# Three pairs of expert slots in rotation, and a tail that adds the last rows in two fp32r parts, in a hybrid diffusion step with 32 routed experts

## The chip, the cores and the metric

The kernel runs as one program on one core of a Trainium2 chip. The metric is the device time of one execution in microseconds (us), as the median of three runs. The engines are TensorE (PE, with PEld for its weight loads), VectorE (DVE), ScalarE (ACT), GpSimd (POOL) and SyncE (SP), which issues most of the transfers; 16 DMA engines carry them. Each engine runs its own list of instructions in order, and the lists are tied together by semaphores alone.

## What is computed

One layer of a diffusion backbone over 128 context tokens and 512 latent tokens of width 1024: normalisation, retention and differential attention, their merge, a residual, and then a mixture of experts and the final norm. The change touches only the last part, which in the reference is:

```python
combine = jnp.einsum('nk,nke->ne', w, jax.nn.one_hot(gidx, N_EXPERTS, dtype=F32))    # top 2 of 32 experts
a = jax.nn.silu(jnp.einsum('nd,edf->nef', hf, wg)) * jnp.einsum('nd,edf->nef', hf, wu)
y = jnp.einsum('nef,efd->nd', a * combine[:, :, None].astype(a.dtype), wd)
...
x = x + g2 * hier_moe(h2, rgw, rgb, rew, reb, wg, wu, wd)
y_prompt = rmsnorm(xp, final_norm_g)
y_sample = rmsnorm(xs, final_norm_g)
```

All inputs and outputs are float32. An expert has three weights of 1 MB each (gate, up and down; 1024 by 256, twice, and 256 by 1024).

## The kernel before

The 640 tokens are five tiles of 128 rows (`NT = 5`; `PT = 4` is the context tile). The residual `x1` stays in SBUF. The normalised rows `h2` are written to a table in DRAM, and routing on the chip gives each expert 64 places. Experts are worked in 16 **pairs** (`PAIRS`), expert 2p and 2p+1 sharing the 128 places of pair p. For each pair:

- POOL gathers the pair's rows from the table (`rows_in`, L2423) into `xg`;
- PE transposes them (`gathered`, L1319), ACT copies them out (L1711);
- PE multiplies by the gate and up weights (`gate_up`, L1326) as soon as `ld_gu` says that they have landed; ACT and DVE form silu times up, times the routing weight (L1716, L2264, L2269);
- PE transposes that (`hidden`, L1332), ACT copies it (L1720), and PE multiplies by the down weights (`down`, L1339);
- DVE multiplies by the modulation row `g2` into `y_out` (`gated_rows`, L2279) and signals `y_d`; POOL scatters `y_out` to the table `y_rows` in DRAM (`rows_out`, L2428) and signals `st_y`. The last pair is not scattered: the tail adds it from `y_out` by a one-hot matrix `last_hot`.

SBUF holds weights of six experts, in **slots** 0 to 5 (`w_gu`, `w_dn`). SP loads them in program order. Pairs 0, 1 and 2 are loaded into slots 0-1, 2-3 and 4-5 ahead of time. Then only slots 0-1 and 2-3 take turns: `next_weights(p, e, slot)` waits until PE is through with the gate and up weights of pair p and loads the next two experts there, then the same for the down weights. Slots 4-5 stand idle from pair 2 until pair 13, whose experts are loaded there after the loop, one expert after the other (gate, up, down of 26, then of 27). Pairs 14 and 15 go to slots 0-1 and 2-3: gate and up of both first (pair 15's in two halves, L918, the second half signalling `ld_rest`), then down of both. PE's code matches this: pairs 3 to 12 are a hardware loop over two pairs, and for pairs 14 and 15 it runs `gate_up` of 15 before `down` of 14.

**The tail.** When all of `y_rows` is stored (`st_y`, waited for by SP at L932) SP loads two rows for each token, `y1` and `y2` (L949, L950), in order of tiles, each pair of them signalling `ld_y[t]`. PE puts into PSUM `last_hot * y_out` (`last_rows`, L1436) and `identity * y2` (`second_rows`, L1441), all in float32, first `last_rows` of four tiles and then `second_rows` of four. For each tile DVE adds `y1` to `x1` (L2331), then PSUM to `x1` (L2333), then multiplies by the final norm's row (L2335); ACT sums the squares (L1762), POOL takes the inverse root (L2401, L2402), ACT scales (L1758) and SP stores (L954).

Code behind `n_over > 0` serves experts with more than 64 rows; it is not entered with these inputs.

## Time and profile before

| what | value |
|---|---|
| median of 3 runs | 1228.64 us (1227.13 to 1230.97) |
| the profiled execution | 1228.74 us, of which the span is 1226.9 us |
| PE busy | 1082.7 us, 88% of the span |
| DVE, ACT, POOL busy | 594.7, 403.2, 104.7 us |
| mean rate of the DMA engines | 184 GB/s over the span |
| moved in the span | 226.09 MB |

The span is the time between the first and the last instruction that the profiler recorded; 1.8 us of the execution lie around it. Busy shares are means over stages with different limits, so the stage that the change touches (from about 950 us to the end) has to be read by itself: who waits there, and for what. Only the waits on the path that ends last cost time.

### The profile page before, as it was taken

The page shows a single profiled execution, that of the slowest core. Times are in us where ns is not written, and L with a number is a line of the kernel's source. Part 1 is how long each engine was busy: PE and PEld are TensorE (multiplying, and loading weights), DVE is VectorE, ACT ScalarE, POOL GpSimd, SP SyncE. Part 2 cuts the span into 40 slices and gives each one's busy share as a digit, 9 for nine tenths or more (in the row PEclk, how much of TensorE's full clock was granted, in tenths as well). Part 3 has the DMA queues.
Part 4 walks back from the last instruction along what each step waited for, and adds up shares of the span by engine and source line. Part 5 has one row for each costly group of instructions (what it writes and reads, how often), then busy time and mean ns, then how long its engine had stood idle before and what let it go on. Part 6 is the DMA issues. An engine that isn't in the chain of part 4 may idle for free.

```text
span 1226.9 us, 13934 instructions
## 1 busy us (share of the span) xinstructions
PE 1082.7 (88%) x5427; PEld 772.2 (63%) x5427; DVE 594.7 (48%) x927; ACT 403.2 (33%) x797; POOL 104.7 (9%) x106
## 2 busy tenths in 40 slices
PE   3999999989999999999998899799993998777785
PEld 2687777777887777777876666687883333222232
DVE  3478525647335454451536665455559322122125
ACT  4441131112245565562236565341331111011103
POOL 1000011111000000000000101000014011111002
PEclk9999999989999999999999999899995999999898
DMA  8757723211421212213230211563618989999966
GB/s 301 263 169 258 263 93 119 71 60 52 146 86 54 92 52 91 82 61 120 77 121 9 66 52 52 216 270 131 240 52 317 388 342 424 421 421 421 417 247 253
DMA packets 72317, 226.09 MB, mean 184 GB/s; under 512 B 9533, under 2 KB 20086, under 8 KB 58562
## 3 DMA queue, kind: packets, MB, share of 16 engines
q1 hardware_dynamic: 64722, 208.35, 46.0%
q0 software_dynamic: 4464, 10.12, 2.2%
q10 hardware_dynamic: 3072, 6.82, 1.5%
q8 instruction: 40, 0.66, 0.2%
q14 instruction: 19, 0.16, 0.0%
HBM read 205.68 MB, written 25.72 MB: 189 GB/s over the span
## 4 chain that ended last, share of the span: by engine, by line
PE 61%; DVE 10%; DMA 9%; issue 8%; ACT 8%; SPq 2%; POOL 1%; ACTq 0%; DVEq 0%; POOLq 0%
PE ps L1090 36%; PE ps L1326 8%; DMA arena<-in_moe_w_up 6%; PE ps L1250 3%; PE ps L1339 3%; ACT arena L1663 3%; DMA arena<-in_w_ada 2%; PE ps L1280 2%; ACT w_high L1482 1%; PE ps L1264 1%; DVE mx L2128 1%; DVE w_low L1833 1%; DVE mx L2129 1%; PE ps L1121 1%; SPq L671 1%
## 5 line engine op out<-in xcount | busy, mean ns | idle before, releaser
L1090 PE MATMUL ps<-w_high,h_high 128*128 128x512 f32 x600 | 242.1, 404 | 5.1 <-DVE arena L1944 2.2
L1090 PE MATMUL ps<-w_high,h_low 128*128 128x512 f32 x600 | 235.6, 393 | 0.0
L1090 PE MATMUL ps<-w_low,h_high 128*128 128x512 f32 x600 | 235.5, 392 | 0.0
L1833 DVE TENSOR_TENSOR w_low<-w_loaded,w_high 128x2048 fp32r<-128x2048 f32 x44 | 100.7, 2289 | 107.2 <-ACT w_high L1482 107.1
L1326 PE MATMUL ps<-arena 128*64 128x512 f32 x512 | 121.5, 630 | 23.5 <-DMA arena<-in_moe_w_up 15.8
L1090 PEld LDWEIGHTS ps<-w_high,h_high 128*128 128x128 f32 x600 | 114.0, 190 | 34.6 <-issue 6.4
L1090 PEld LDWEIGHTS ps<-w_high,h_low 128*128 128x128 f32 x600 | 113.8, 190 | 24.8
L1090 PEld LDWEIGHTS ps<-w_low,h_high 128*128 128x128 f32 x600 | 114.1, 190 | 22.5
L1482 ACT CAST w_high<-w_loaded 128x2048 fp32r<-128x2048 f32 x44 | 84.0, 1910 | 76.6 <-DMA w_loaded<-in_w_in 42.9
L1326 PEld LDWEIGHTS ps<-arena 128*64 128x64 f32 x512 | 39.1, 145 | 103.6 <-issue 103.2
L1591 ACT COPY arena<-ps 128x512 f32<-128x512 f32 x55 | 32.3, 587 | 168.0 <-PE ps L1090 168.0
L1663 ACT ACTIVATE arena<-ps,neg_mx 128x768 f32<-128x768 f32 (+1 forms) x80 | 62.9, 792 | 41.1 <-DVE neg_mx L2130 40.9
L1716 ACT ACTIVATE arena<-ps 128x256 f32<-128x256 f32 x16 | 6.2, 385 | 196.4 <-PE ps L1326 196.4
L2264 DVE SCALAR_TENSOR_TENSOR arena<-arena,ps 128x256 f32<-128x256 f32 x16 | 6.7, 421 | 128.1 <-ACT arena L1716 128.1
L1339 PE MATMUL ps<-arena 128*64 128x512 f32 x256 | 58.4, 598 | 9.9 <-ACT arena L1720 8.7
L1250 PE MATMUL ps<-arena 64*128 64x256 f32 (+2 forms) x288 | 54.7, 494 | 7.2 <-ACT arena L1663 5.7
L2128 DVE TENSOR_REDUCE mx<-ps 128x1 f32<-128x768 f32 (+1 forms) x40 | 32.8, 821 | 40.9 <-PE ps L1250 40.9
L1280 PE MATMUL ps<-arena 128*128 128x128 f32 x384 | 48.0, 275 | 0.0
L1280 PEld LDWEIGHTS ps<-arena 128*128 128x128 f32 x384 | 46.4, 192 | 1.1
L1886 DVE SCALAR_TENSOR_TENSOR arena<-arena 128x2048 f32<-128x2048 f32 x20 | 45.8, 2346 | 1.4 <-DMA arena<-in_w_ada 1.4
L2279 DVE TENSOR_TENSOR arena<-ps,arena 128x1024 f32<-128x1024 f32 x16 | 19.6, 1224 | 53.7 <-PE ps L1339 29.7
L1264 PE MATMUL ps<-const,arena 128*128 128x128 f32 x200 | 30.8, 286 | 16.5 <-ACT ps L1680 14.1
(300 smaller groups left out, 1657.8 us busy)
## 6 DMA issues: line engine op xcount, KB each, us to landing
arena<-in_moe_w_down SPq DMA_DIRECT2D x32, 1024.0 KB, 19.4
arena<-in_moe_w_gate SPq DMA_DIRECT2D x30, 1024.0 KB, 13.4
arena<-in_moe_w_up SPq DMA_DIRECT2D x30, 1024.0 KB, 18.0
w_loaded<-in_w_in SPq DMA_DIRECT2D x27, 1024.0 KB, 5.9
arena<-in_w_ada SPq DMA_DIRECT2D x24, 1024.0 KB, 5.7
w_loaded<-in_w_in ACTq DMA_DIRECT2D x5, 1024.0 KB, 7.4
y_rows<-arena SPq DMA_DIRECT2D x10, 512.0 KB, 7.0
gates<-arena SPq DMA_DIRECT2D x20, 256.0 KB, 2.0
```

The costliest lines, as they stand in the source:

```text
L1090: mm = pe.matmul(out, x[:, t, kk * P:(kk + 1) * P], w[w_buf(i)][:, k, :], start=(begins and k == 0 and j == 0), stop=(k == HK - 1 and j == ...
L1250: mm = pe.matmul(score[c][:, lo:hi], qT[h % 2][r, t * P:(t + 1) * P], keys, start=True, stop=True, skip_group_check=True)
L1264: mm = pe.transpose(B(6 + k // 4)[:, (k % 4) * P:(k % 4 + 1) * P], mixed[:, k * P:(k + 1) * P], ident)
L1280: mm = pe.matmul(pv_out, mixedT[s % 2][:, k * P:(k + 1) * P], v, start=(k == 0), stop=(k == 5))
L1326: mm = pe.matmul(B(bank_at)[BLK * i:BLK * (i + 1), :].rearrange("p (g f) -> p g f", g=2), xgT[slot][:, k, BLK * i:BLK * (i + 1)], w_gu[e0 ...
L1339: mm = pe.matmul(B(5 + n)[BLK * i:BLK * (i + 1), :], act_aT[slot][:, k, BLK * i:BLK * (i + 1)], w_dn[e0 + i][:, k, n * N512:(n + 1) * N512 ...
L1482: act.copy(w_hi[w_buf(i)][:], w_raw[w_buf(i)]).then_inc(w_rounded, 1)
L1591: free(act.copy(dst[:, t, c0:c0 + N512], src), n)
L1663: act.activation(probs[:, c, 0:n], score[c][:, 0:n], ACT.Exp, bias=neg_mx[:, s % 2, c:c + 1], scale=DH ** -0.5, accum_out=den[:, s % 2, c: ...
L1833: dve.tensor_tensor(w_lo[b][:], w_raw[b], w_hi[b][:].bitcast(F32), ALU.subtract).then_inc(w_split, 1)
L1886: ins = dve.scalar_tensor_tensor(out=total, in0=ada_place[i % 2], scalar=ccol[:, k, s:s + 1], in1=total, op0=ALU.mult, op1=ALU.add)
L2128: dve.tensor_reduce(mx[:, 0:1], score[0][:, 0:n], AXX, ALU.max)
```

## The change

It does four things.

1. The six slots rotate as three pairs of slots: pair p uses slots 2(p mod 3) and the next, throughout. SP's loop becomes written-out code: for p from 3 to 14 it waits until PE is through with the gate and up weights of pair p-3, loads those of p, waits for the down product of pair p-3, loads the down weights of p. Pair 15 has its halves as before, in slots 0-1. PE's loop is written out as well.
2. PE's order at the end: pair 14 is an ordinary pair, and pair 15 follows it whole. DVE and ACT follow suit.
3. `y1`, `y2` and `fin_row` get other places in SBUF. The load of `fin_row` waits for the down product of pair 13 and no longer for its gate and up product.
4. The tail: ACT rounds the last pair's rows to fp32r (`y_high`, two halves), DVE makes the rest (`y_low`), and `last_rows` is now two fp32r products, with `y_high` and `y_low`, in place of one in float32. In each tile `second_rows` comes first; the order on PE is second 0, second 1, last 0, last 1, then second and last tile by tile. DVE adds `y1` two tiles ahead.

```diff
-        fin_row = at(162, D)
-        y1, y2 = tiles(28, NT, D), tiles(48, NT, D)
+        fin_row = at(102, D)
+        y1, y2 = tiles(118, NT, D), tiles(158, NT, D)
+        y_high, y_low = split_at("y_high", 86, 1, D), split_at("y_low", 90, 1, D)
...
-        last_hot = masks[:, 0:NT * P]
+        last_hot = nc.alloc_sbuf_tensor_at("last_hot", [P, NT * P], F32R, offset=masks_base)
...
+            for p in range(3, PAIRS - 1):
+                slot = 2 * (p % 3)
+                sp.wait_ge(pe_gu, p - 2)
                 for i in range(2):
-                    load_gate_up(e + i, slot + i)
-                sp.wait_ge(pe_dn, p + 1)
+                    load_gate_up(2 * p + i, slot + i)
+                sp.wait_ge(pe_dn, p - 2)
                 for i in range(2):
-                    load_down(e + i, slot + i)
-
-            next_weights(0, 6, 0)
-            next_weights(1, 8, 2)
-            with sp.Fori(0, (PAIRS - 8) // 2) as i:
-                next_weights(2 * i + 3, 4 * i + 10, 0)
-                next_weights(2 * i + 4, 4 * i + 12, 2)
-
-            for e, slot in ((NE - 6, 4), (NE - 5, 5)):
-                load_expert(e, slot)
-            sp.wait_ge(pe_gu, PAIRS - 4)
-            for i in range(2):
-                load_gate_up(NE - 4 + i, i)
...
-            sp.wait_ge(pe_gu, PAIRS - 2)
+            sp.wait_ge(pe_dn, PAIRS - 2)
             sp.dma_start(fin_row, a["final_norm_g"].partition_broadcast(P)).then_inc(ld_fin, 16)
...
+            for p in range(PAIRS - 1):
+                pair(p, p % 2, 2 * (p % 3), p // 2, p // 3, first=(p == 0))
...
-            def last_rows(t):
-                for n in range(2):
-                    pe.matmul(B(2 * t % 8 + n), last_hot[:, t * P:(t + 1) * P], y_out[:, 1, n * N512:(n + 1) * N512], start=True, stop=False)
-
             def second_rows(t):
                 pe.wait_ge(ld_y[t], 16 + 32)
                 for n in range(2):
-                    mm = pe.matmul(B(2 * t % 8 + n), ident, y2[:, t, n * N512:(n + 1) * N512], start=False, stop=True)
+                    pe.matmul(B(2 * t % 8 + n), ident, y2[:, t, n * N512:(n + 1) * N512], start=True, stop=False, skip_group_check=True)
+
+            def last_rows(t):
+                for n in range(2):
+                    c = slice(n * N512, (n + 1) * N512)
+                    pe.wait_ge(y_split, split_before + n + 1)
+                    for y in (y_high, y_low):
+                        mm = pe.matmul(B(2 * t % 8 + n), last_hot[:, t * P:(t + 1) * P], y[:, 0, c], start=False, stop=(y is y_low), skip_group_check=True)
                 mm.then_inc(pe_sum, 1)
...
+            second_rows(0)
+            second_rows(1)
+            last_rows(0)
+            last_rows(1)
+            pe.wait_ge(y_d, PAIRS)
+            for t in range(2, PT):
+                second_rows(t)
                 last_rows(t)
-            for t in range(PT):
-                second_rows(t)
             pe.wait_ge(x2_ready, 1)
+            second_rows(PT)
             last_rows(PT)
-            second_rows(PT)
...
+            act.wait_ge(y_d, PAIRS)
+            for n in range(2):
+                c = slice(n * N512, (n + 1) * N512)
+                act.copy(y_high[:, 0, c], y_out[:, 1, c]).then_inc(y_rounded, 1)
...
+                dve.tensor_tensor(y_low[:, 0, c], y_out[:, 1, c], y_high[:, 0, c].bitcast(F32), ALU.subtract).then_inc(y_split, 1)
...
+            first_rows(0)
+            first_rows(1)
             dve.wait_ge(ld_fin, 16 * 3)
             for t in range(NT):
-                dve.wait_ge(ld_y[t], 16 + 32)
-                link(dve.tensor_tensor(x1[:, t, :], x1[:, t, :], y1[:, t, :], ALU.add))
-                dve.wait_ge(pe_sum, t + 1)
-                dve.tensor_tensor(x1[:, t, :], x1[:, t, :], psf[:, (2 * t % 8) * N512:(2 * t % 8 + 2) * N512], ALU.add).then_inc(x2_ready, 1)
-                dve.wait_ge(x2_ready, t + 1)
-                dve.tensor_tensor(y1[:, t, :], x1[:, t, :], fin_row, ALU.mult).then_inc(fin_scaled, 1)
+                last_sum(t)
+                if t + 2 < NT:
+                    first_rows(t + 2)
+                scaled_by_norm(t)
```

On PE, the end of the expert stage, from pair 13's `gate_up` to pair 15's `down`, reads as follows before (L1326 `gate_up`, L1319 `gathered`, L1332 `hidden`, L1339 `down`):

```order
L1326 MATMUL ps<-arena 64x512 x16
L1319 MATMUL ps<-const,arena 128x128 x8
L1332 MATMUL ps<-const,arena 128x128 x2
L1339 MATMUL ps<-arena 64x512 x8
L1326 MATMUL ps<-arena 64x512 x16
L1319 MATMUL ps<-const,arena 128x128 x8
L1332 MATMUL ps<-const,arena 128x128 x2
L1326 MATMUL ps<-arena 64x512 x16
L1339 MATMUL ps<-arena 64x512 x8
L1332 MATMUL ps<-const,arena 128x128 x2
L1339 MATMUL ps<-arena 64x512 x8
```

The same stretch of the changed kernel (L1316 `gate_up`, L1309 `gathered`, L1322 `hidden`, L1329 `down`):

```order
L1316 MATMUL ps<-arena 64x512 x16
L1309 MATMUL ps<-const,arena 128x128 x8
L1322 MATMUL ps<-const,arena 128x128 x2
L1329 MATMUL ps<-arena 64x512 x8
L1316 MATMUL ps<-arena 64x512 x16
L1309 MATMUL ps<-const,arena 128x128 x8
L1322 MATMUL ps<-const,arena 128x128 x2
L1329 MATMUL ps<-arena 64x512 x8
L1316 MATMUL ps<-arena 64x512 x16
L1322 MATMUL ps<-const,arena 128x128 x2
L1329 MATMUL ps<-arena 64x512 x8
```

Pair 14's `down` has moved ahead of pair 15's `gate_up`. On SP, the loads behind the loop, that is for pairs 13, 14 and 15, stood before as follows (L793 gate and up, L796 down, L918 the halves of pair 15):

```order
L793 DMA arena<-in_moe_w_gate 128x2048
L793 DMA arena<-in_moe_w_up 128x2048
L796 DMA arena<-in_moe_w_down 128x2048
L793 DMA arena<-in_moe_w_gate 128x2048
L793 DMA arena<-in_moe_w_up 128x2048
L796 DMA arena<-in_moe_w_down 128x2x1024
...
L918 DMA arena<-in_moe_w_gate 128x1024
L918 DMA arena<-in_moe_w_up 128x1024
L796 DMA arena<-in_moe_w_down 128x2048 x4
L927 DMA arena<-in_final_norm_g 128x1024
```

In the changed kernel the same stretch, from the down weights of pair 13 on, is (L797 gate and up, L800 down, L911 the halves):

```order
L800 DMA arena<-in_moe_w_down 128x2048 x2
L797 DMA arena<-in_moe_w_gate 128x2048
L797 DMA arena<-in_moe_w_up 128x2048
L797 DMA arena<-in_moe_w_gate 128x2048
L797 DMA arena<-in_moe_w_up 128x2048
L800 DMA arena<-in_moe_w_down 128x2048
L800 DMA arena<-in_moe_w_down 128x2x1024
L911 DMA arena<-in_moe_w_gate 128x1024
...
L800 DMA arena<-in_moe_w_down 128x2048 x2
L917 DMA arena<-in_final_norm_g 128x1024
```

Pair 14's two down loads now stand ahead of pair 15's gate and up loads, and only pair 15's two down loads stand behind those. In the tail, DVE's rows from the first sum on were before (L2331 adds `y1`, L2333 adds PSUM, L2335 multiplies), three for each of five tiles, of which the first two tiles are shown:

```order
L2331 TENSOR_TENSOR arena<-arena 128x1024
L2333 TENSOR_TENSOR arena<-arena,ps 128x1024
L2335 TENSOR_TENSOR arena<-arena 128x1024
L2331 TENSOR_TENSOR arena<-arena 128x1024
L2333 TENSOR_TENSOR arena<-arena,ps 128x1024
L2335 TENSOR_TENSOR arena<-arena 128x1024
```

and of the changed kernel (L2313, L2317, L2321 the same three), up to the second tile's product:

```order
L2313 TENSOR_TENSOR arena<-arena 128x1024 x2
L2317 TENSOR_TENSOR arena<-arena,ps 128x1024
L2313 TENSOR_TENSOR arena<-arena 128x1024
L2321 TENSOR_TENSOR arena<-arena 128x1024
L2317 TENSOR_TENSOR arena<-arena,ps 128x1024
L2313 TENSOR_TENSOR arena<-arena 128x1024
L2321 TENSOR_TENSOR arena<-arena 128x1024
```

Two additions of `y1` now stand ahead of the first sum with PSUM, so that from the start of the first of those sums to the start of the last DVE has eleven instructions to run, where it had twelve.

## Rows read from the trace of the kernel before

**Rows 1.** The page, second part: 40 equal slices of 30.7 us.

```profile
PEclk9999999989999999999999999899995999999898
GB/s 301 263 169 258 263 93 119 71 60 52 146 86 54 92 52 91 82 61 120 77 121 9 66 52 52 216 270 131 240 52 317 388 342 424 421 421 421 417 247 253
```

**Rows 2.** Three stretches: length; PE busy, instructions; clock; DMA share; GB/s.

```profile
992.00:1001.00 9.00, 8.34 (x44) 1.00 0.51 163
1001.00:1179.00 178.00, 142.05 (x643) 0.95 1.02 419
1179.00:1191.00 12.00, 10.90 (x52) 1.00 0.31 128
```

**Rows 3.** The timeline of PE's gate and up products (start, length, what, idle before).

```profile
1048.34 8.78 PE L1326 MATMUL ps<-arena 128*64 128x512 f32 x32 [3.03 <-DMA arena<-in_moe_w_up]
1065.69 7.09 PE L1326 MATMUL ps<-arena 128*64 128x512 f32 x32 [1.96 <-DMA arena<-in_moe_w_up]
1153.66 9.06 PE L1326 MATMUL ps<-arena 128*64 128x512 f32 x32 [6.35 <-issue]
```

**Rows 4.** Pair 14's up weights, second expert: its issue and landing.

```profile
L793 SPq DMA_DIRECT2D arena<-in_moe_w_up x1: 3198/3198/3198, 1139.8 to 1139.8; - x1
...
DMA to landing us min/median/max: 28.4/28.4/28.4
```

**Rows 5.** Pair 15's last up half: its issue and landing.

```profile
L918 SPq DMA_DIRECT2D arena<-in_moe_w_up x1: 2141/2141/2141, 1160.5 to 1160.5; - x1
...
DMA to landing us min/median/max: 19.0/19.0/19.0
```

**Rows 6.** The scatters of pairs 3 to 13, and that of pair 14.

```profile
L2428 POOL DMA_INDIRECT y_rows<-arena,to_idx x11: 1011/1011/1011, 1007.1 to 1170.6; - x11
DMA to landing us min/median/max: 7.9/8.5/8.9
L2428 POOL DMA_INDIRECT y_rows<-arena,to_idx x1: 1923/1923/1923, 1190.3 to 1190.3; - x1
DMA to landing us min/median/max: 4.2/4.2/4.2
```

**Rows 7.** The timeline from 1165 us on, its main steps.

```profile
1165.36 3.65 PE L1339 MATMUL ps<-arena 128*64 128x512 f32 x16 [0.46 <-ACT arena L1720]
1170.63 1.01 POOL L2428 DMA_INDIRECT y_rows<-arena,to_idx  x1 [19.25 <-DVE arena L2279]
1178.14 7.09 PE L1326 MATMUL ps<-arena 128*64 128x512 f32 x32 [0.18 <-ACT arena L1711]
1190.26 1.92 POOL L2428 DMA_INDIRECT y_rows<-arena,to_idx  x1 [18.62 <-DVE arena L2279]
1193.88 1.22 DVE L2279 TENSOR_TENSOR arena<-ps,arena 128x1024 f32<-128x1024 f32 x1 [2.57 <-PE ps L1339]
1194.73 0.33 SPq L949 DMA_DIRECT2D arena<-y_rows  x1
1201.20 1.23 DVE L2331 TENSOR_TENSOR arena<-arena 128x1024 f32<-128x1024 f32 x1 [6.10 <-DMA arena<-y_rows]
1202.54 5.71 PE L1441 MATMUL ps<-arena,const 128*128 128x512 f32 x12
1204.52 1.22 DVE L2333 TENSOR_TENSOR arena<-arena,ps 128x1024 f32<-128x1024 f32 x1 [2.10 <-PE ps L1441]
1219.12 1.22 DVE L2333 TENSOR_TENSOR arena<-arena,ps 128x1024 f32<-128x1024 f32 x1
```

**Rows 8.** The second load of tile 1, `y2`: its issue and landing.

```profile
L950 SPq DMA_DIRECT2D arena<-y_rows x1: 433/433/433, 1196.1 to 1196.1; - x1
...
DMA to landing us min/median/max: 7.6/7.6/7.6
```

**Rows 9.** PE in a dense stretch where all is fp32r products (L1090).

```profile
560.00:570.00 10.00, 10.00 (x46) 1.00 0.22 84
```

**Rows 10.** The queue that brings instructions: packets, MB, share.

```profile
q8 instruction: 40, 0.66, 0.2%
```

More of the change, by code:

```diff
@@ L282, in build @@
         lam_s, neg_lam = sb("lam_s", [P, 2]), sb("neg_lam", [P, 1])
+        masks_base = -(-nc.sbuf_base // 32) * 32
         masks = sb("masks", [P, 12 * P])
@@ L917, in _ @@
                     for g, w in enumerate((a["moe_w_gate"], a["moe_w_up"])):
-                        sp.dma_start(w_gu[2 + i][:, g, ks, :], w[0, NE - 2 + i].rearrange("(p k) f -> p k f", p=P)[:, ks, :]).then_inc(ld_rest if half else ld_gu[2 + i], 16)
-            sp.wait_ge(pe_dn, PAIRS - 4)
-            for i in range(2):
-                load_down(NE - 4 + i, i)
+                        sp.dma_start(w_gu[i][:, g, ks, :], w[0, NE - 2 + i].rearrange("(p k) f -> p k f", p=P)[:, ks, :]).then_inc(ld_rest if half else ld_gu[i], 16)
             sp.wait_ge(pe_dn, PAIRS - 3)
             for i in range(2):
-                load_down(NE - 2 + i, 2 + i)
-            sp.wait_ge(pe_gu, PAIRS - 2)
+                load_down(NE - 2 + i, i)
+            sp.wait_ge(pe_dn, PAIRS - 2)
             sp.dma_start(fin_row, a["final_norm_g"].partition_broadcast(P)).then_inc(ld_fin, 16)
@@ L1373, in _ @@
             gathered(0).then_inc(pe_xt, 1)
-            pair(0, 0, 0, 0, 0, first=True)
-            pair(1, 1, 2, 0, 0)
-            pair(2, 0, 4, 1, 0)
-            with pe.Fori(0, (PAIRS - 6) // 2) as i:
-                pair(2 * i + 3, 1, 0, i + 1, i + 1)
-                pair(2 * i + 4, 0, 2, i + 2, i + 1)
-            h = PAIRS // 2 - 1
-            pair(PAIRS - 3, 1, 4, h - 1, 1)
-            a_p, b_p = PAIRS - 2, PAIRS - 1
-            for i in (0, 1):
-                pe.wait_ge(ld_gu[i], 32 * h)
-            pe.wait_ge(xt_read, a_p + 1)
-            gate_up(0, 0, 2).then_inc(pe_gu, 1)
-            pair_gathered(b_p, 1, h)
-            pe.wait_ge(gu_act, a_p + 1)
-            hidden(0).then_inc(pe_aT, 1)
-            pe.wait_ge(xt_read, b_p + 1)
-            for i in (2, 3):
-                pe.wait_ge(ld_gu[i], 32 * h)
+            for p in range(PAIRS - 1):
+                pair(p, p % 2, 2 * (p % 3), p // 2, p // 3, first=(p == 0))
+            p = PAIRS - 1
+            for i in (0, 1):
+                pe.wait_ge(ld_gu[i], 32 * (p // 3) + 32)
+            pe.wait_ge(xt_read, p + 1)
             for half in range(2):
@@ L1396, in _ @@
                     pe.wait_ge(ld_rest, 64)
-                mm = gate_up(1, 2, 3, range(HK * half, HK * half + HK))
+                mm = gate_up(1, 0, 3, range(HK * half, HK * half + HK))
             mm.then_inc(pe_gu, 1)
-            pe.wait_ge(aT_read, a_p + 1)
+            pe.wait_ge(gu_act, p + 1)
+            hidden(1).then_inc(pe_aT, 1)
+            pe.wait_ge(aT_read, p + 1)
             for i in (0, 1):
-                pe.wait_ge(ld_dn[i], 16 * h)
-            pe.wait_ge(y_d, a_p)
-            down(0, 0).then_inc(pe_dn, 1)
-            pe.wait_ge(gu_act, b_p + 1)
-            hidden(1).then_inc(pe_aT, 1)
-            pe.wait_ge(aT_read, b_p + 1)
-            for i in (2, 3):
-                pe.wait_ge(ld_dn[i], 16 * h)
-            pe.wait_ge(y_d, b_p)
-            down(1, 2).then_inc(pe_dn, 1)
+                pe.wait_ge(ld_dn[i], 16 * (p // 3) + 16)
+            pe.wait_ge(y_d, p)
+            down(1, 0).then_inc(pe_dn, 1)
             n_over = pe.value_load(n_ov[0:1, 0:1], min_val=0, max_val=OVER)
-            pe.wait_ge(y_d, PAIRS)
             with pe.If(n_over > 0):
+                pe.wait_ge(y_d, PAIRS)
                 with pe.Fori(0, OVER // 2) as j:
@@ L2301, in _ @@
             pair(1, 1, 0, first=True)
-            with dve.Fori(1, PAIRS // 2 - 1) as i:
+            with dve.Fori(1, PAIRS // 2) as i:
                 for par in range(2):
                     pair(2 * i + par, par, i)
-            for par in range(2):
-                pair_act(PAIRS - 2 + par, par)
-            for par in range(2):
-                pair_rows(PAIRS - 2 + par, par, PAIRS // 2 - 1)
+            for n in range(2):
+                c = slice(n * N512, (n + 1) * N512)
+                dve.wait_ge(y_rounded, rounded_before + n + 1)
+                dve.tensor_tensor(y_low[:, 0, c], y_out[:, 1, c], y_high[:, 0, c].bitcast(F32), ALU.subtract).then_inc(y_split, 1)
             n_over = dve.value_load(n_ov[0:1, 0:1], min_val=0, max_val=OVER)
```

16 lines of the change are left out of this document (13 added, 3 removed).

## The prediction

> **What bounds the kernel now.** I read the page's slices first, then the granted clock and DMA share by stretches, then the timeline of the last 80 us, and last the landing times of single transfers. The slices show two regimes: TensorE at full clock and 50 to 270 GB/s mostly up to slice 30, and from slice 34 to 38 some 421 GB/s in every slice, and 0.8 is the lowest granted clock of a slice behind slice 31 [rows 1]. Between 1001 and 1179 us all 16 DMA engines are busy (share 1.02) at 419 GB/s, while PE is busy 142 of 178 us [rows 2]. That stage waits for weights: `gate_up` of pair 7 had PE idle for 3.03 us until an up weight landed, and then took 8.78 us in place of 7.09, because the granted clock had fallen to its lower level (1.2 GHz) [rows 3]. So a PE that is done sooner gains nothing there; a DMA engine that is busy sooner does.
>
> Ahead of that stage lies a hole. From 992 to 1001 us the DMA share is 0.51 at 163 GB/s [rows 2]: slots 4-5 are free after pair 2, but SP loads nothing into them. The lost DMA time is 9.0 x (1 - 0.51/1.02) = 4.5 us.
>
> The end is a chain through three engines. Pair 14's scatter is issued at 1190.26 and lands 4.2 us later [rows 6, 7]; the first load of `y1` leaves at 1194.73; tile 0 can be added at 1201.20; the first sum with PSUM starts at 1204.52, the last at 1219.12, and from there 7.8 us of square, root, scale and store lead to the span's end [rows 7]. I call the start of the first `y1` load **Y**. It is late because pair 14's `down` stands behind pair 15's `gate_up` (1178.14 to 1185.2).
>
> **The change, step by step.**
>
> *Filled hole.* After the change pair 5 is loaded when pair 2's `gate_up` is done, with pairs 3 and 4 still in the queue, so the hole closes and every later weight moves forward. Mean over the engines: 4.5 us. But engines differ: at the end they run out over 12 us (share 0.31 from 1179 to 1191 [rows 2]), and a transfer has landed only when its slowest engine is through. The slowest ones had less of a hole to fill. Bounds 0 and 4.5; I take s = 4.0, near the upper end, because the hole is longer than the spread could have become in a stage this short before it.
>
> The Trainium skill (DMA: Bandwidth & Descriptors, section "Latency and other measured facts") says that DMA engines 7 and 15 are usually slower than the others in traces. That would agree with the tail of the share; by it s would be well under the mean hole, and the forecast would come out up to 4 us later, which is rival B.
>
> *Pair 14.* Its last gate/up transfer landed at 1139.8 + 28.4 = 1168.2 [rows 4]. The bytes ahead of it are the same in both orders, so it lands at 1164.2, and `gate_up` starts at 1164.4 (pair 13's weights, now gate and up first, are no obstacle). From a start of `gate_up` to the issue of the scatter there is 7.09 us [rows 3], then about 2.6 us to `down`, 3.65 us of `down` [rows 7], and 1.7 us to DVE's product and POOL's issue. For pair 13, cold, it was 1170.63 - 1153.66 = 17.0 us [rows 3, 7]; less the 2.0 us by which its `gate_up` was long (9.06 against 7.09), 15.0 us. The scatter is issued at 1164.4 + 15.0 = 1179.4. If PE idles 3 us or more ahead of it and the clock falls, 1.7 us later. The wait of about 3 us per pair at 16 to 17 us for weights against 13 us for work decides this; in the trace cold and warm pairs take turns [rows 3]. I take half: 1180.2.
>
> *The scatter's flight.* Between 7.9 and 8.9 us with busy DMA engines, 4.2 us when they are nearly idle [rows 6]. Now it falls into the stretch in which engines run out one after the other (1179 to 1191 us before, so about 1175 to 1187). Bounds 4.2 and 8.9; I take 7.2, nearer the busy end, because it has landed only when the slowest engine has carried its part. With the 0.27 us from landing to issue (1190.26 + 4.2 = 1194.46 to 1194.73), Y = 1180.2 + 7.2 + 0.3 = 1187.7. That is 7.0 us earlier.
>
> *Pair 15 must not be later than that.* Its last up half landed at 1160.5 + 19.0 = 1179.5 with 4.2 MB of down weights behind it [rows 5]; now 2.1 MB of those are ahead, 5.0 us at 419 GB/s, so 1179.5 + 5.0 - 4.0 = 1180.5. `gate_up` starts when `down` of 14 is over, at 1164.4 + 7.1 + 2.6 + 3.65 = 1177.8 (warm) or 1179.5 (cold); its second half 3.5 us later, so nothing waits. `down` of 15 then ends at about 1191.2 to 1192.9 (before: 1193.8), DVE's product 1.3 us later. ACT's two copies and DVE's two subtractions, of 512 columns each at some 0.6 us, are done by 1194 to 1196. In the new order they are needed when `second_rows` of tiles 0 and 1 are through, after 1197. Cost 0; had Y come at 1184 they would begin to show.
>
> *The start of the tail.* The loads of `y1` and `y2` are the same 5.2 MB. Before, the first sum started at Y + 9.8. Now `last_rows(0)` stands behind `second_rows(1)`, and that waits for tile 1, which lands at 1196.1 + 7.6 = 1203.7, that is Y + 9.0 [rows 8]. Then `second_rows(1)`: 12 instructions take 5.71 us for three tiles [rows 7], so 1.8 us with the drain; then four fp32r products of 10/46 = 0.22 us each [rows 9], 0.9 us. Mixing fp32 and fp32r in one PSUM bank has no row; a bound is one more weight load, 0.2 us at most against nothing; I take 0.1. First sum at Y + 11.8: 2.0 us dearer. The saved work (1.8 us of fp32 `last_rows` per tile becomes 0.9) no longer stands on the path, since PE waited for DVE there from tile 1 on.
>
> *The rest of the tail.* From first to last sum DVE ran 12 instructions in 14.60 us, 1.217 each [rows 7]; now 11, 13.4 us. Gain 1.2. The last tile's chain behind it is unchanged: square, root, scale, store.
>
> *Written-out loops, new places in SBUF, the later `fin_row`.* Nothing: PE waits for weights all the same, `fin_row` is needed only after Y + 13.
>
> **Sum** against the profiled execution (1228.74 us, 0.1 above the median of the runs, so the difference carries over): Y earlier by 7.0, tail 2.0 - 1.2 = 0.8 dearer, gain 6.2. Forecast 1228.7 - 6.2 = **1222.5 us**.
>
> **Rivals.** The measurement can tell about 0.3%, 3.7 us, from no change.
>
> *A. As forecast, with another clock or flight.* Warm pair and a scatter at 4.2 us: Y = 1179.4 + 4.5 = 1183.9. The tail then waits for y_low a little (0.5 us); gain 10.8 - 0.8 - 0.5 = 9.5, 1219.2. Cold pair and 8.9 us: Y = 1181.1 + 9.2 = 1190.3, gain 3.6, 1225.1. Chance of this family 0.70, some of it at its slow end under 3.7 us.
>
> *B. The hole does not count (s = 0), or only in part.* The slowest DMA engines had no hole, so pair 14's weights land at 1168.2. Then the scatter is issued at 1184.2, Y = 1191.7, gain 3.0 - 0.8 = 2.2; pair 15's second half waits until 1184.5, which is not in the way. 1226.5, and 1227.3 with a cold pair in place of half of one. For it: the long tail of the share [rows 2]. Against: 9 us at half share is more than a few engines' idleness. Chance 0.18.
>
> *C. Slower: instruction loading.* PE's loop over pairs is now ten pairs written out, so PE draws new code while the DMA engines are full. Before, 40 packets carried 0.66 MB [rows 10]. A transfer on another queue takes 8.5 us in that stage against 4.2 outside it [rows 6]. If PE stood still for 8.5 us at a block of code in pair 14 or 15, Y or pair 15 would be 8.5 us later: 1222.5 + 8.5 = 1231.0. It decides for slower from a stall of 6.2 us on; one in pair 3 to 12 is hidden by the wait for weights. Against: the mixers ran through straight code at full share (PE busy 10.00 of 10.00 us [rows 9]), and from 1001 to 1179 us a delay of a few us has slack to hide in. Chance 0.06. The Trainium skill (Runtime: NRT & Kernel Launch, section "Instruction fetch mechanics") says the opposite of the rival: the sequencer fetches the next block while it runs the present one, so that straight code hides the fetch, and a taken branch out of the window is what stalls. By that page C costs 0 and the forecast stands; no row of before shows straight PE code with full DMA engines for long.
>
> *D. Slower: the clock stays low at the end.* PE has gaps in pairs 13 to 15 and between the tiles. If the clock were at 1.2 GHz from pair 14's `gate_up` on, work of 7.1 + 0.9 + 3.65 us up to the scatter would double, Y later by 11.6 us: 1234. It decides for slower when more than 6.2 us of PE work ahead of Y, or in the tail, runs cold. Against: from 1001 to 1179 us the mean clock is 0.95 [rows 2], and a cold `gate_up` recovered within itself (9.06, not 14.2 [rows 3]). Chance 0.06.
>
> **Numbers.** A and B are on one side. Faster by over 0.3%: 0.68 (A but its slow end, a sliver of B); within: 0.21; slower: 0.11. The range takes in A whole and B, 1218.5 to 1227.3, and leaves out C and D.
>
> **What would show it.** DMA share 1.0 from 992 to 1001 us. Pair 14's `gate_up` at about 1164.4, the scatter's issue at 1179 to 1182 with a landing of 5 to 9 us, first `y1` load near 1188, first sum with PSUM 11.8 us after it, last sum 13.4 us after the first. Idle PE in front of every `gate_up` from about pair 7 on. Wrong it would be if the weights of pair 14 landed no earlier, if PE stood idle in the written-out pairs with its weights there, or if the first sum came more than 14 us after Y.

## The result, and the profile after

| | before | changed |
|---|---|---|
| median of 8 runs each | 1226.2 us (1224.76 to 1230.97) | 1219.89 us (1214.03 to 1222.71) |
| ratio, with its 95% interval | | 0.9937 (0.9922 to 0.9952) |
| the profiled execution | 1228.74 us | 1219.85 us |
| its span | 1226.9 us | 1218.0 us |

By the ratio the change makes the kernel 0.63% faster (0.48 to 0.78%), some 7.7 us of 1227 (5.9 to 9.6 us). The two medians alone differ by 6.3 us, which lies within that interval. The forecast was 6.2 us less than the profiled execution, and that execution lay 2.5 us above the median which more runs of the kernel before gave. So the forecast time, 1222.5 us, is 2.6 us above the measured one. Three executions behind the experiments (two of the kernel before, one of O) took 1414 to 1598 us and stand in no ratio.

Two rows of the changed kernel's profile answer to [rows 1], and one to [rows 10]:

```profile
PEclk9999999989999999999999999899996899999898
GB/s 306 273 164 257 261 96 111 80 61 52 147 87 36 112 53 64 111 52 130 70 80 59 58 61 44 156 271 203 201 45 338 342 422 420 419 421 419 418 283 246
...
q8 instruction: 44, 0.72, 0.2%
```

Slice 33 now has 422 GB/s where it had 342, and four more packets of code were fetched. The stretches show where the higher rate comes from; columns as in [rows 2]:

```profile
992.00:1001.00 9.00, 7.88 (x42) 1.00 1.01 420
1001.00:1172.00 171.00, 139.29 (x638) 0.96 1.02 417
1172.00:1186.00 14.00, 11.80 (x56) 1.00 0.42 168
1186.00:1200.00 14.00, 10.73 (x37) 1.00 0.96 373
```

The hole from 992 to 1001 us is gone (share 1.01, was 0.51), and the DMA engines run out some 5 us earlier: from 1174 on, not from 1179. From 1186 on they carry `y1` and `y2`, which before started at 1194.73. Of the transfers behind [rows 4, 5, 6, 8], these are pair 14's last up weights, pair 15's last up half, pair 14's scatter and the second load of tile 1:

```profile
L797 SPq DMA_DIRECT2D arena<-in_moe_w_up x1: 2909/2909/2909, 1132.6 to 1132.6; - x1
DMA to landing us min/median/max: 29.4/29.4/29.4
L911 SPq DMA_DIRECT2D arena<-in_moe_w_up x1: 2087/2087/2087, 1161.4 to 1161.4; - x1
DMA to landing us min/median/max: 16.8/16.8/16.8
L2423 POOL DMA_INDIRECT y_rows<-arena,to_idx x1: 1004/1004/1004, 1177.1 to 1177.1; - x1
DMA to landing us min/median/max: 7.6/7.6/7.6
L940 SPq DMA_DIRECT2D arena<-y_rows x1: 433/433/433, 1186.4 to 1186.4; - x1
DMA to landing us min/median/max: 7.4/7.4/7.4
```

Issue plus landing gives 1162.0, 1178.2, 1184.7 and 1193.8 us. The timeline of the same steps as in [rows 7] (L1316 `gate_up`, L2317 adds PSUM):

```profile
1144.93 9.52 PE L1316 MATMUL ps<-arena 128*64 128x512 f32 x32 [3.99 <-issue]
1162.04 7.09 PE L1316 MATMUL ps<-arena 128*64 128x512 f32 x32 [1.29 <-issue]
1175.25 7.04 PE L1316 MATMUL ps<-arena 128*64 128x512 f32 x32
1177.13 1.00 POOL L2423 DMA_INDIRECT y_rows<-arena,to_idx  x1 [13.77 <-DVE arena L2262]
1185.03 0.34 SPq L939 DMA_DIRECT2D arena<-y_rows  x1
1196.87 1.22 DVE L2317 TENSOR_TENSOR arena<-arena,ps 128x1024 f32<-128x1024 f32 x1 [1.76 <-PE ps L1416]
1209.84 1.21 DVE L2317 TENSOR_TENSOR arena<-arena,ps 128x1024 f32<-128x1024 f32 x1
```

Two distances matter here. From Y (1185.03) to the first sum with PSUM (1196.87) it is 11.84 us, where it was 9.79; from there to the last sum 12.97 us, where it was 14.60. The chain that ended last says why Y matters: it starts with pair 14's scatter and goes over tile 1's second load (L1409 `second_rows`, L1416 `last_rows`).

```profile
1177.13 7.65 DMA y_rows<-arena,to_idx
...
1186.36 7.43 DMA arena<-y_rows
...
1193.83 1.98 PE ps L1409 x4
1195.82 0.93 PE ps L1416 x4
```

**Where each execution starts the stage.** Pair 1's `gate_up` starts at 965.63 us in the profile before and at 964.00 in that after, though nothing ahead of it is changed. Over all profiles shown below it lies between 959.81 and 965.63. So 1.6 us of the 8.9 us between the two spans are not the change's, and 7.3 us are, which agrees with the ratio. To compare two profiles I count from pair 1's `gate_up`: Y is 229.1 us behind it before and 221.0 us after, that is 8.1 us earlier.

### The profile page after: what moved, and what is told of

Read it like the earlier page. It is cut to its first block and busy times, and to the rows that moved or that the text cites. A ratio compares the mean times of both kernels' runs of the same rounds, so it can differ in the third digit from the quotient of the medians.

```text
span 1218.0 us, 13831 instructions
## 1 busy us (share of the span) xinstructions
PE 1078.1 (89%) x5427; PEld 774.0 (64%) x5427; DVE 595.8 (49%) x929; ACT 404.5 (33%) x799; POOL 103.2 (8%) x106
## 5 line engine op out<-in xcount | busy, mean ns | idle before, releaser
L1316 PE MATMUL ps<-arena 128*64 128x512 f32 x512 | 120.9, 627 | 20.7 <-issue 19.4
L1316 PEld LDWEIGHTS ps<-arena 128*64 128x64 f32 x512 | 41.6, 144 | 98.4 <-issue 98.1
L1329 PE MATMUL ps<-arena 128*64 128x512 f32 x256 | 58.5, 598 | 8.1 <-ACT arena L1699 8.1
```

What stands on the lines that cost most here:

```text
L1316: mm = pe.matmul(B(bank_at)[BLK * i:BLK * (i + 1), :].rearrange("p (g f) -> p g f", g=2), xgT[slot][:, k, BLK * i:BLK * (i + 1)], w_gu[e0 ...
L1329: mm = pe.matmul(B(5 + n)[BLK * i:BLK * (i + 1), :], act_aT[slot][:, k, BLK * i:BLK * (i + 1)], w_dn[e0 + i][:, k, n * N512:(n + 1) * N512 ...
```

## The experiments

The theory under test, theory 1: the rotation gains by the filled hole; end order and tail gain only together, since the early `y1` load is of use only when the tail no longer begins with work that needs pair 15's rows. Its rival: the tail's cheaper products, or the order alone, are the gain. R, O and T stand for rotation, end order and tail. Every ratio is against the kernel before, run on the same chip; 1 us is 0.08%. The diffs are shortened (`...` marks what is left out), and the comments behind code in them are mine.

### R alone

The changed kernel without its end order and tail:

```diff
+                if p == PAIRS - 2:
+                    continue              # pair 14's down loads go behind pair 15's gate and up
...
+            gate_up(0, 4, 2).then_inc(pe_gu, 1)      # pair 14
+            pair_gathered(b_p, 1, h)
...
+            hidden(0).then_inc(pe_aT, 1)
...                                                  # gate_up of pair 15
+            down(0, 4).then_inc(pe_dn, 1)            # pair 14
...
-            second_rows(0)
-            second_rows(1)
-            last_rows(0)
-            last_rows(1)
...
+            for t in range(PT):
                 last_rows(t)                         # float32, from y_out
+            for t in range(PT):
+                second_rows(t)
```

> Three-pair rotation alone, with the end order (pair 15's gate and up ahead of pair 14's down) and the tail of before; y1, y2 and fin_row at the places of the changed kernel. Theory 1 (the filled hole moves every later weight forward by its 4.5 us of DMA time): 4 to 4.5 us faster than before, no hole at 992 to 1001 us, first y1 load 4 to 4.5 us earlier. Theory 2 (the slowest DMA engines had no hole, the gain is the tail's): within 1 us of before.

Measured: 0.9954 (0.9936 to 0.9972), 5.6 us faster (3.4 to 7.9). The first `y1` load and the first sum (L2322):

```profile
1188.46 0.34 SPq L943 DMA_DIRECT2D arena<-y_rows  x1
1198.25 1.22 DVE L2322 TENSOR_TENSOR arena<-arena,ps 128x1024 f32<-128x1024 f32 x1 [2.11 <-PE ps L1430]
```

Y is 6.3 us earlier than before, with pair 1's start 1.35 us earlier, so 4.9 us of it are the rotation's. From Y to the first sum it is 9.79 us and from there to the last 14.60, both as before. Theory 1 holds: the rotation alone is worth about 5 us.

### O alone

```diff
+            sp.wait_ge(pe_dn, PAIRS - 4)
+            for i in range(2):
+                load_down(NE - 4 + i, i)      # ahead of pair 15's gate and up, no longer behind
...
-            gate_up(0, 0, 2).then_inc(pe_gu, 1)
-            pair_gathered(b_p, 1, h)
...
-            hidden(0).then_inc(pe_aT, 1)
...
+            pair(PAIRS - 2, 0, 0, h, h - 1)
...
                 mm = gate_up(1, 2, 3, range(HK * half, HK * half + HK))
...
-            down(0, 0).then_inc(pe_dn, 1)
```

> Only the end order is changed: pair 14 whole, then pair 15, and SP loads pair 14's down weights ahead of pair 15's gate and up. Two-pair rotation and float32 tail stay. Theory 1: first y1 load about 4 to 5 us earlier (near 1190), but pair 15 ends 1.5 to 2 us later, and the old tail's four last_rows wait for it, so the first sum is 1 to 1.5 us later: slower by about 1 us. Theory 2 (the order alone brings the early y loads and with them the gain): 3 us or more faster.

Measured: 1.0018 (1.0006 to 1.0030), 2.2 us slower. The timeline (L949 first `y1` load, L1426 the float32 `last_rows`, L2319 sum with PSUM):

```profile
1189.04 0.34 SPq L949 DMA_DIRECT2D arena<-y_rows  x1
1196.45 7.13 PE L1426 MATMUL ps<-arena,masks 128*128 128x512 f32 x16 [1.79 <-DVE arena L2269]
1205.41 1.22 DVE L2319 TENSOR_TENSOR arena<-arena,ps 128x1024 f32<-128x1024 f32 x1 [7.80 <-PE ps L1431]
```

Y came 5.7 us earlier in the profile; 2.8 us of that are an earlier pair 1 (962.87), so the order moved Y by 2.9 us. The scatter's issue moved by 6.0 us, and 3.1 of them went into its flight: from issue to Y it is now 7.52 us, where it was 4.47. What Y gained was lost again: 7.13 us of `last_rows` wait for pair 15's rows until 1196.45, DVE waits 7.80 us for PE, and the first sum comes 16.37 us after Y. The rival, that the early loads alone are the gain, has fallen.

### T alone

```diff
-            for t in range(PT):
-                last_rows(t)
-            for t in range(PT):
-                second_rows(t)
+            second_rows(0)
+            second_rows(1)
+            last_rows(0)              # two fp32r products
+            last_rows(1)
```

> Only the tail is changed (fp32r parts, second_rows first, y1 added two tiles ahead). Rotation and end order stay. Theory 1: the last rows are not what the tail waits for when y1 and y2 load late: first sum 2.0 us later after the first y1 load, 1.4 us less from first to last sum, so 0.4 to 0.8 us slower than before. Theory 2 (the tail's cheaper products are the gain): 3 us or more faster.

Measured: 1.0001 (0.9987 to 1.0014), no change. The first `y1` load and the first sum (L2353):

```profile
1194.42 0.33 SPq L953 DMA_DIRECT2D arena<-y_rows  x1
1206.57 1.22 DVE L2353 TENSOR_TENSOR arena<-arena,ps 128x1024 f32<-128x1024 f32 x1 [2.75 <-PE ps L1448]
```

From Y to the first sum it is 12.15 us, from there to the last (1219.54) 12.97: 2.4 dearer and 1.6 cheaper. The scatter also took 1.1 us longer from issue to Y than before (5.54 against 4.47); no run shows why. The rival that the cheaper products are the gain has fallen too.

### The hole put back

```diff
                 slot = 2 * (p % 3)
-                sp.wait_ge(pe_gu, p - 2)
+                sp.wait_ge(pe_gu, 4 if p == 5 else p - 2)
```

> The changed kernel with the hole put back: pair 5's gate and up loads wait for pair 3's gate and up product, as before the change, and no longer for pair 2's. Theory 1: 4 to 4.5 us slower than the changed kernel, that is 3 to 3.5 us faster than before; DMA share near 0.5 from about 990 to 999 us. Theory 2: as fast as the changed kernel, 7.7 us faster than before.

Measured: 0.9972 (0.9959 to 0.9985), 3.4 us faster than before, so 4.3 us slower than the changed kernel. The hole is there again, some 6 us earlier in the program's time, since the stage began earlier in this execution (length, clock, DMA share, GB/s):

```profile
985.00:994.00 9.00, 1.00 0.54 211
```

This one wait in SP's list is worth about what the DMA engines lost in idle time: s = 4.3 us by the ratios (each is uncertain by 0.13 to 0.15%, so the difference by some 2.4 us), where 4.0 was forecast and 4.5 was the mean over the engines. The profiles say 4.7: pair 14's `gate_up` starts 202.8 us behind pair 1's (1162.58 and 959.81), in the changed kernel 198.0.

### R and O, without T

The changed kernel with the float32 tail of before.

```diff
-        last_hot = nc.alloc_sbuf_tensor_at("last_hot", [P, NT * P], F32R, offset=masks_base)
+        last_hot = masks[:, 0:NT * P]
...
-            second_rows(0)
-            second_rows(1)
-            last_rows(0)
-            last_rows(1)
+            for t in range(PT):
+                last_rows(t)
+            for t in range(PT):
+                second_rows(t)
```

> The changed kernel with the tail of before (float32 one-hot products, last_rows of four tiles first, y1 added tile by tile). Theory 1: the four last_rows wait for pair 15's rows and take 7.1 us, so the first sum comes no earlier than about 1199 us (8.5 us behind pair 15's last DVE product): 4 us slower than the changed kernel, 3.5 us faster than before. Theory 2 (the three parts add up, and the tail alone gave nothing): as the changed kernel.

Measured: 0.9969 (0.9958 to 0.9980), 3.8 us faster than before. Its timeline (L938 first `y1` load, L1407 `last_rows`, L2300 first sum):

```profile
1183.77 0.34 SPq L938 DMA_DIRECT2D arena<-y_rows  x1
1189.06 7.13 PE L1407 MATMUL ps<-arena,masks 128*128 128x512 f32 x16 [1.79 <-DVE arena L2250]
1198.02 1.22 DVE L2300 TENSOR_TENSOR arena<-arena,ps 128x1024 f32<-128x1024 f32 x1 [7.80 <-PE ps L1412]
```

The first sum comes 14.25 us after Y, not 11.84, and the last 14.60 us after the first, not 12.97. The tail, worth nothing by itself, is worth 3.9 us here by the ratios, 4.0 by these distances.

### O and T, without R

Both edits above on the kernel before.

```diff
+            pair(PAIRS - 2, 0, 0, h, h - 1)       # the edit of O
...
+            second_rows(0)                        # the edit of T
+            second_rows(1)
+            last_rows(0)
+            last_rows(1)
```

> End order and tail of the changed kernel, with the two-pair rotation of before. Theory 1: order and tail gain only together: first y1 load 4 to 5 us earlier than before, and the new tail can use it; 3 to 4 us faster than before. Theory 2 (parts add up: order 2.2 us slower alone, tail 0.1): 2 us slower than before.

Measured: 0.9980 (0.9968 to 0.9992), 2.4 us faster. O (+2.2) and T (+0.1) would add up to 2.3 us slower; together they gain. The size is under the 3 to 4 us that I expected. From Y (1185.91) to the first sum (1197.81) it is 11.90 us, where O alone had 16.37.

### R and T, without O

```diff
                 for i in range(2):
                     load_gate_up(2 * p + i, slot + i)
+                if p == PAIRS - 2:
+                    continue              # pair 14's down loads go behind pair 15's gate and up
...
-            for p in range(PAIRS - 1):
+            for p in range(PAIRS - 2):    # then gate_up of 15 ahead of down of 14, as before
```

> Rotation and tail of the changed kernel, end order of before. Theory 1 (the new tail gains only where the first y1 load is ahead of pair 15's last rows): as the rotation alone, 5 to 6 us faster than before, 2 us slower than the changed kernel. Theory 2 (tail and rotation gain together too): as the changed kernel, 7.7 us faster.

Measured: 0.9979 (0.9966 to 0.9993), 2.6 us faster, and not the 5 to 6 that theory 1 wanted. Its timeline and R's (L1427, and in R L1430, are `second_rows`; the row of the stretch has length, PE busy, clock, DMA share, GB/s):

```profile
1187.73 0.34 SPq L944 DMA_DIRECT2D arena<-y_rows  x1
1192.95 5.30 PE L1427 MATMUL ps<-arena,const 128*128 128x512 f32 x8 [7.20 <-DMA arena<-y_rows]
1199.32 1.22 DVE L2339 TENSOR_TENSOR arena<-arena,ps 128x1024 f32<-128x1024 f32 x1 [2.53 <-PE ps L1434]
...
1193.00:1195.00 2.00, 2.00 (x3) 0.50 1.02 416
```

```profile
1189.29 7.13 PE L1425 MATMUL ps<-arena,masks 128*128 128x512 f32 x16 [1.78 <-DVE arena L2268]
1196.26 5.70 PE L1430 MATMUL ps<-arena,const 128*128 128x512 f32 x12
```

In R the float32 `last_rows` fill the wait for the first loads. With T that wait is empty: PE idles for 7.20 us, begins again at a granted clock of 0.50 and takes 5.30 us for eight instructions of which R runs twelve in 5.70. That is not where the time goes, though: the first sum comes 11.59 us after Y, no later than in the changed kernel (11.84), and from Y to the last sum it is 24.56 us, in R 24.39. In these two profiles, counted from pair 1 (962.45 and 964.28), R and T ends 1.3 us later than R, and 1.0 of it is the scatter, 5.50 us from issue to Y against 4.47, as in T alone; the cause of that is open. By the ratios (0.9954 and 0.9979) it is 3.1 us, but the two intervals overlap.

### PE's pairs as a loop

```diff
-            for p in range(PAIRS - 1):
-                pair(p, p % 2, 2 * (p % 3), p // 2, p // 3, first=(p == 0))
+            for p in range(3):
+                pair(p, p % 2, 2 * (p % 3), p // 2, p // 3, first=(p == 0))
+            with pe.Fori(0, 2) as i:
+                for j in range(6):
+                    pair(6 * i + 3 + j, (3 + j) % 2, 2 * (j % 3), 3 * i + (3 + j) // 2, 2 * i + 1 + j // 3)
```

> The changed kernel with PE's pairs 3 to 14 as a hardware loop of two turns over six pairs, in place of written-out code; the order of work is the same. Instruction loading hidden: within 0.5 us of the changed kernel. If new code were loaded late while the DMA engines are full, this kernel would differ from it by 2 us or more, one way or the other.

Measured: 0.9940 (0.9925 to 0.9955), median 1219.80 us. That is the changed kernel's time within 1.8 us. 41 packets of code were fetched and not 44. The stall of 6.2 us or more on which rival C of the prediction rested is not there. In this profile pair 14's `gate_up` was a cold one and pair 15's `down` too, and the first sum came 12.53 us after Y:

```profile
1159.63 8.78 PE L1316 MATMUL ps<-arena 128*64 128x512 f32 x32 [2.10 <-DMA arena<-in_moe_w_up]
1184.22 5.35 PE L1329 MATMUL ps<-arena 128*64 128x512 f32 x16 [0.46 <-ACT arena L1702]
1195.84 1.22 DVE L2320 TENSOR_TENSOR arena<-arena,ps 128x1024 f32<-128x1024 f32 x1
```

No wait stands in front of that sum: here DVE, which had to make `y_low` first, was the one that came last, and not tile 1's landing.

### Filler for the clock

```diff
                 pair(p, p % 2, 2 * (p % 3), p // 2, p // 3, first=(p == 0))
+                if 6 <= p <= 13:
+                    for _ in range(3):
+                        pe.matmul(B(7)[:, 0:388], ident, const[:, 0:388], start=True, stop=True)
```

> The changed kernel with three products of no use (identity by 388 columns of constants, into an unused PSUM bank) behind the down product of each of pairs 6 to 13, in TensorE's wait for weights, about 1.9 us per pair. Clock theory: half of the gate and up products run at the lower clock because PE stood idle for 3 us or more before them; with the gap cut by 1.9 us those of pairs 13 and 14 take 7.1 us every time, so the first y1 load comes up to 1.7 us earlier and the median is 0.5 to 1.5 us below the changed kernel's, with less spread. Rival (the end hangs on the weights alone, or the filler holds PE up): within 0.5 us, or slower.

Measured: 0.9938 (0.9924 to 0.9951), median 1220.04 us: no gain. The filler did what it should:

```profile
1145.15 7.09 PE L1316 MATMUL ps<-arena 128*64 128x512 f32 x32 [1.82 <-issue]
1158.46 2.22 PE L1368 MATMUL ps<-const 128*128 128x388 f32 x6
1162.27 7.09 PE L1316 MATMUL ps<-arena 128*64 128x512 f32 x32 [1.59 <-issue]
```

Every `gate_up` from pair 7 to 14 takes 7.09 us, pair 13's too (9.52 in the changed kernel), and pair 14's still starts when its weights land, 198.1 us behind pair 1's against 198.0. So the clock in pairs 7 to 13 is paid out of the wait for weights. In pair 14 it is not: that pair was warm in the changed kernel's profile, and cold (8.78 us) in those of the hole put back, the loop and the tile-by-tile kernel below. In the latter two, counted from pair 1, Y came 0.8 and 1.0 us later than in the changed kernel. If that happens in half of the executions the filler should give back some 0.5 us (an estimate from these profiles), which is less than the interval of 1.6 us can tell.

### Tile by tile

```diff
             second_rows(0)
-            second_rows(1)
             last_rows(0)
+            second_rows(1)
             last_rows(1)
...
             first_rows(0)
-            first_rows(1)
             for t in range(NT):
                 last_sum(t)
-                if t + 2 < NT:
-                    first_rows(t + 2)
+                if t + 1 < NT:
+                    first_rows(t + 1)
                 scaled_by_norm(t)
```

> The changed kernel with the tail tile by tile: PE second 0, last 0, second 1, last 1; DVE adds y1 one tile ahead and not two. Theory 1: the first sum no longer waits for tile 1 (2.6 us behind tile 0), DVE starts it right behind its first addition, some 3 us earlier, and has 13 operations of 1.18 us to run from its first addition to its last sum: last sum about 2 us earlier, 2 us faster than the changed kernel. Rival: DVE waits for each tile's landing or for PE, within 0.5 us of the changed kernel.

Measured: 0.9927 (0.9910 to 0.9945), median 1219.68 us (1216.54 to 1221.37). By the ratios that is 1.2 us under the changed kernel where 2 were expected, and within the intervals. Its profile shows a stretch that missed the gain:

```profile
1186.90 5.35 PE L1329 MATMUL ps<-arena 128*64 128x512 f32 x16 [0.46 <-ACT arena L1699]
1196.00 1.23 DVE L2313 TENSOR_TENSOR arena<-arena 128x1024 f32<-128x1024 f32 x1 [0.45 <-issue]
1197.26 1.22 DVE L2317 TENSOR_TENSOR arena<-arena,ps 128x1024 f32<-128x1024 f32 x1
```

Pair 14's `gate_up` was a cold one here (8.78 us), pair 15's `down` took 5.35 us in place of 3.65, and DVE's first addition, which stands behind `y_low`, came at 1196.00, so late that the first sum was 11.12 us after Y. Here the tail hangs on pair 15.

### Tile by tile, with the filler

The edits of the last two sections together.

```diff
+                        pe.matmul(B(7)[:, 0:388], ident, const[:, 0:388], start=True, stop=True)
...
             second_rows(0)
             last_rows(0)
             second_rows(1)
```

> Tile-by-tile tail and filler together. If the tail of the tile-by-tile kernel was held up by pair 15 coming late at the lower clock, and the filler keeps the clock up, the last sum comes 2 us earlier than in the changed kernel: 2 to 3 us faster than it. If the filler does nothing: as the tile-by-tile kernel, within 1 us of the changed kernel.

Measured: 0.9924 (0.9911 to 0.9937), median 1217.73 us (1216.81 to 1219.93), the lowest of all. In its profile the first sum follows the first addition with no wait between them:

```profile
1184.13 0.33 SPq L939 DMA_DIRECT2D arena<-y_rows  x1
1191.43 1.23 DVE L2316 TENSOR_TENSOR arena<-arena 128x1024 f32<-128x1024 f32 x1 [0.45 <-issue]
1192.69 1.22 DVE L2320 TENSOR_TENSOR arena<-arena,ps 128x1024 f32<-128x1024 f32 x1
```

The first sum is 8.6 us after Y and no longer 11.8; from there to the last it is 14.1 us and not 13.0, as DVE has one more addition to run, so the last sum is 2.1 us earlier behind Y. Against the filler alone, measured beside it, the time is 0.14% lower, 1.7 us, and that is within the two intervals. It is the best version seen, and not proven better than the changed kernel.

### fin_row behind tile 1

```diff
-            sp.wait_ge(pe_dn, PAIRS - 2)
-            sp.dma_start(fin_row, a["final_norm_g"].partition_broadcast(P)).then_inc(ld_fin, 16)
...
                 sp.dma_start(y2[:, t, :], y_dram[(NT + t) * P:(NT + t + 1) * P, :]).then_inc(ld_y[t], 16)
+                if t == 1:
+                    sp.dma_start(fin_row, a["final_norm_g"].partition_broadcast(P)).then_inc(ld_fin, 16)
...
+                if t == 0:
+                    dve.wait_ge(ld_fin, 16 * 3)      # ahead of the first product, no longer of the first sum
```

> The changed kernel with the load of fin_row behind tile 1's y1 and y2, out of the queue in which pair 14's scatter flies. If its 0.5 MB hold up the scatter: first y1 load up to 1 us earlier and the median up to 1 us lower; tile 2 lands 1.2 us later relative to it, which DVE just does not feel. If not: within 0.5 us.

Measured: 0.9940 (0.9927 to 0.9953), no change. From the scatter's issue (1175.89) to Y (1183.31) it is 7.42 us, where the changed kernel has 7.90. Such a half us is too small for these runs: their interval is 1.6 us.

## Why the prediction was right and where it was off

All seven subsets of the three parts were run. The gain by the ratios, and the distances in each profile (pair 1 is the start of its `gate_up`), in us:

| | gain | pair 1 to Y | Y to first sum | first to last sum | last sum to end |
|---|---|---|---|---|---|
| before | 0 | 229.1 | 9.8 | 14.6 | 7.8 |
| T | -0.1 | 230.5 | 12.2 | 13.0 | 7.8 |
| O | -2.2 | 226.2 | 16.4 | 14.6 | 7.8 |
| R | 5.6 | 224.2 | 9.8 | 14.6 | 8.2 |
| O and T | 2.4 | 226.1 | 11.9 | 13.0 | 7.8 |
| R and O | 3.8 | 221.0 | 14.3 | 14.6 | 8.2 |
| R and T | 2.6 | 225.3 | 11.6 | 13.0 | 8.2 |
| all three | 7.7 | 221.0 | 11.8 | 13.0 | 8.2 |

The parts do not add up (3.3 against 7.7), and the gap is the mechanism that the prediction's sum followed step by step without naming it: O brings the loads forward, T lets the tail use them (from Y to the first sum 16.4 and 14.3 us with O but without T, 11.8 to 11.9 with both).

- **The filled hole.** Right in place, and too small. Pair 14's weights landed 202.6 us behind pair 1's start before (1168.2) and 198.0 after (1162.0): s = 4.6 against 4.0, and the run with the hole put back gives 4.3 by the ratios, 4.7 by its profile. That is the whole mean of 4.5. Rival B (s = 0) is out, and so is the thought that s stays under the mean because the slowest engines had less of a hole. No view here shows single engines, so what each of them did is not shown.
- **Pair 14.** `gate_up` started as soon as its weights had landed (0.2 us less than I had put), and from there to the scatter's issue it took 15.1 us (1162.04 to 1177.13), the warm value of 15.0. I had taken half of a cold pair's 1.7 us; this pair was warm. The condition that I had put on it does not hold up: a wait of 3 us or more ahead of a product does not decide its clock. In the changed kernel a `gate_up` behind 3.06 us of waiting ran warm, with the hole put back one behind 2.04 us ran cold, and there the one before it had been cold too:

```profile
1127.56 7.09 PE L1316 MATMUL ps<-arena 128*64 128x512 f32 x32 [3.06 <-issue]
...
1162.58 8.78 PE L1316 MATMUL ps<-arena 128*64 128x512 f32 x32 [2.04 <-issue]
```

- **The scatter's flight.** 7.9 us from issue to Y against 7.5 forecast. Behind a cold pair 14 it was shorter: 6.9 us in the loop's profile, 7.0 in the tile-by-tile kernel's. So pair and flight together were 23.0 us here and 23.7 to 23.8 there, and the forecast 23.3 lies between them.
- **Y.** 221.0 us behind pair 1's start against 222.1 forecast, so 8.1 us earlier than before in place of 7.0.
- **Pair 15.** Its last half landed at 1178.2, with its `gate_up` under way since 1175.25: no wait, as forecast, though its second half was due only some 0.5 us later. In the loop's profile its cold `down` did cost the tail 0.7 us.
- **The start of the tail.** 11.84 against 11.8, by two misses that cancel: tile 1 landed 8.8 us after Y and not 9.0, and from there to the first sum it took 3.1 us and not 2.8, since four instructions of `second_rows` take 1.98 us. Of the bound for mixed fp32 and fp32r products in a bank nothing shows: four fp32r products took 0.93 us in the chain.
- **First to last sum.** 12.97 against 13.4. From one DVE instruction's start to the next it is 1.25 us where the second waits for the first one's result, and 1.14 where it does not. Before, each tile had two such waits, now it has one, since `y1` of another tile is added between a sum and its product. And it was not DVE that PE waited for in the tail of before, as the prediction has it: PE's only wait from the first sum on was 0.58 us for `y2`, while DVE ran without a pause.
- **Last sum to the end.** I had called this chain unchanged and the new places free. It is 8.16 us and was 7.78. In all ten profiles with the rotation it is 8.1 to 8.2 us, in the four without it 7.8; the last store is issued 4.5 us behind the last sum before and after, and lands 3.2 us later in place of 2.9. The two groups differ in SP's written-out loads and in the places in SBUF, among others, and no run parts these, so the cause stays open.
- **Rivals C and D.** No stall for code, by the loop. The clock did fall for pair 14's `gate_up` in three of the profiles of variants and for pair 15's `down` in some, but for single products; it moved Y by about 1 us and not by 11.6.

Two steps failed. The first is the base of the sum: "0.1 above the median of the runs, so the difference carries over". Three runs gave 1228.64 us; eight gave 1226.2, and beside the experiments the median was 1227.0 to 1228.1. In the profiled execution the stage began late, pair 1 at 965.63 us, later than in any other profile here. Taken from 1226.2 us, the same gain of 6.2 us would have given 1220.0.

The second is in the gain. The term of the filled hole was put at 4.0 us, under the mean, on the ground that the slowest DMA engines had less of a hole to fill; the profiles show 4.6. With it the other terms give the profile's gain: Y was earlier by 8.1 us and not 7.0 (0.6 the hole, 0.2 the start of `gate_up`, 0.7 the warm pair, less 0.4 for the flight), the tail 0.4 us dearer and not 0.8, and the chain behind the last sum, put at nothing, 0.4 us dearer: 7.3 us, where 6.2 was forecast. The ratio's 7.7 us has an interval from 5.9 to 9.6, so the runs by themselves do not tell the two apart. That the forecast gain came so near is in part luck: the warm pair, the flight and the two halves of the tail's start erred in opposite ways.

## What to carry to other kernels

Where the DMA engines are the bound, look for the slices in which they are not busy, far ahead of the end: one wait in SP's list was worth some 4.3 us of 1227. A transfer that is made earlier is worth something only when what stands first in the next stage doesn't wait for something else; measure such edits in pairs, since each alone can read as zero or worse. Compare profiles from a common point near the stage that changed: here their starts differed by more than most of the effects. And ask how far a profiled execution lies from the median of many runs before a forecast of half a per cent is hung on it.

## What the runs showed of the hardware

- TensorE began again at a granted clock of 0.50 (the lower of its two levels) after 7.20 us idle, and eight float32 instructions took 5.30 us, where twelve took 5.70 behind work that had kept PE going. With filler in the waits all `gate_up` products of pairs 7 to 14 took 7.09 us; the time did not change within 1.6 us.
- The length of the wait just ahead does not tell the clock: a `gate_up` behind 3.06 us of waiting took 7.09 us (changed kernel), and one behind 2.04 us took 8.78 (hole put back, where all from pair 7 to 14 were cold).
- The start of the stage differed by up to 5.8 us (959.81 to 965.63 for pair 1) between profiled executions of code that is the same up to there.
- A scatter of POOL took 7.9 to 8.9 us to land while weights were streaming before the change, and 7.2 to 9.4 us over the 15 of the changed kernel; pair 14's took 4.2 us with the DMA engines nearly idle [rows 6], and in the two kernels with T but without O 5.2 to 5.3 us.
